# Prompt stick-breaking attention: operands and outputs turned in the unused columns of the diagonal steps' score slots

## The chip, the cores and the metric

One core of a Trainium2 chip runs the whole kernel. The metric is device time of one execution in microseconds. The engines are TensorE (PE in the profile, its weight loads PEld), VectorE (DVE), ScalarE (ACT), GpSimd (POOL) and SyncE (SP), which issues most transfers. Each works through its own instructions in order and waits for others by semaphores. TensorE writes its results to PSUM, a memory of 8 banks with 512 float32 columns each per partition. The granted clock (PEclk) is a share of TensorE's full speed: 1.0 is 2.4 GHz, 0.5 is 1.2 GHz.

## The reference

One step of a decoder layer, with a prompt of 2048 tokens and 8 samples of 4 new tokens. The input is projected to two groups of heads; the first attends by stick-breaking, the second in dilated windows; then come an output projection and a gated embedding. The part at hand is stick-breaking attention over the prompt, 8 heads of 64:

```python
def _stick_breaking(q, k, v, q_pos, k_pos, bias):
    z = jnp.einsum('bqhd,bkhd->bhqk', q, k).astype(jnp.float32) / math.sqrt(HEAD_DIM)
    z = z + bias.astype(jnp.float32)[None, :, None, None]
    mask = (k_pos[None, :] < q_pos[:, None])[None, None]
    log_1m = jnp.where(mask, jax.nn.log_sigmoid(-z), 0.0)
    rest = lax.cumsum(log_1m, axis=3, reverse=True) - log_1m
    a = jnp.where(mask, jnp.exp(jax.nn.log_sigmoid(z) + rest), 0.0)
    return jnp.einsum('bhqk,bkhd->bqhd', a.astype(v.dtype), v)
```

For each query the weight of a key is its sigmoid times the product of (1 - sigmoid) over all keys between it and the query, which is a sum of softplus values in the exponent.

## The kernel before

`build` runs seven stages one after the other on the core: projection of mixer A, projection of mixer B, prompt stick-breaking, dilated prompt, sampled stick-breaking, dilated sample, merge. Between stages all engines meet. The change is in the third (function `stick_breaking_prompt`), in the helper that loads its operands, and in the line of the second stage that calls that helper.

The stage handles its 8 heads in 4 pairs (`PAIRS`). For a pair, the queries and keys of all 2048 positions lie as rows in the buffer `held`. They are turned by TensorE (a product with the identity matrix into PSUM), then ScalarE copies the result as a rounded high part `T_hi` and VectorE subtracts it for a low part `T_lo`. This is a **fill**. There are 4 fills a pair, each of 8 tiles of 128 x 128, two for the queries and two for the keys.

The scores are made transposed: keys on partitions, queries on columns. The queries are taken in 4 **quarters** of 512 (Q = 0 to 3). A quarter Q passes over the key tiles from its last one, j = 4Q + 3, down to 0: 4, 8, 12 and 16 **steps**, 40 a pair and 160 in all, numbered g. The first four steps of each quarter are its **diagonal**: there key tile j meets only the queries behind it, so columns from `first_col(g)` = 384, 256, 128 and 0 are used and those left of it are not.

A step g does the following, for both heads of the pair at once:

- TensorE, `score(g)`: bias and three products of high and low parts into a **slot** of `Z` (two banks, one for each head); on a diagonal also a mask.
- ScalarE: `exp(g)` (the line called L812 below), then `ln(g)` (L817). VectorE: `softplus(g, h)` (L739). GpSimd: `high(g)`, the softplus rounded (L697). VectorE: `low(g, h)`, the rest (L745).
- TensorE, `sums(g)`: adds the softplus sums within the key tile into the same slot (L894, L898); `totals(g)`: the totals of the tile for the later steps (L909).
- ScalarE, `weights(g)`: exponential of the slot (L824), which frees it; `left(g)`: exponential of the totals (L832).
- TensorE, `weigh(g)`: weights times values into `L` (L922). VectorE, `scale(g)` and `add(g)`: adds it to the quarter's output in `acc`.

When a quarter is done its output is turned back by four transposes (an output **turn**, L864), which ScalarE copies to `o_out` (the put-out, L803).

`Z` has three slots (`ZS = 3`), six of the eight PSUM banks; `total` and `L` hold the other two. Before the change, a list `SLOTS` holds steps, fills and turns in one order, and the n-th entry takes slot n % 3. Every engine runs through this list in a loop over k: it starts entry k + 2 and finishes entry k. So scores run two entries ahead of sums, and a fill or turn is an entry like a step. A fill of the next pair stands before steps 8, 16, 24 and 32 of a pair (`FILL_AT`), the four of the first pair before step 0; a turn stands five steps behind the last step of its quarter (`TURN_AT`). A new entry waits until the slot's last user has been read (`wait_free`): for a step until its weights are out (`a_done`).

SP issues the loads. The rows of the next pair are loaded into `held` when all four fills of the pair are turned. The first pair's are loaded at the end of the projection stage, before the loads of its last item.

## Time and profile before

| | |
|---|---|
| timed runs | 3353.92, 3348.5, 3353.68 us; median 3353.68 us |
| profiled execution, span from first to last instruction | 3201.8 us |
| TensorE busy | 2899.0 us (91%) |
| VectorE busy | 1654.1 us (52%) |
| ScalarE busy | 1464.1 us (46%) |
| GpSimd busy | 632.9 us (20%) |
| mean granted clock of TensorE | 0.953 |
| prompt stick-breaking, first to last compute instruction | 801.6 to 1489.2 us |

The span holds only the time between the first and the last instruction; the timed runs are longer by what lies around it. For the profiled execution the page gives the span alone. The shares are means over seven stages with different limits, so only what is read inside the stage says something of this change. In a row of the timeline the first number is the start and the second the duration, both in microseconds, of the instructions named; x8 means eight of one kind in a row, and the brackets give the idle time of the engine before it and what ended it.

### The profile page before, as it was taken

The numbers are of one execution on the slowest core, as the hardware profiler recorded it, in microseconds if no ns is written. First come the engines' busy times: TensorE is split into PE (matmuls) and PEld (weight loads), VectorE is DVE, ScalarE is ACT, GpSimd is POOL, SyncE is SP. The second block draws the span as 40 slices with busy tenths as digits, with TensorE's granted clock in tenths as the row PEclk, the third lists the DMA queues.
The fourth block names the chain that finished last, engine by engine and source line by source line (L and its number), as shares of the span: only waits on it lengthen the run. The fifth ranks groups of instructions, "written<-read, shape, count | busy, mean of one in ns | idle before, by whom it ended". The sixth has DMA issues, their size and how long they took to land. (4 is left out here: it accounts for less than half of the span.)

```text
span 3201.8 us, 46967 instructions
## 1 busy us (share of the span) xinstructions
PE 2899.0 (91%) x17542; PEld 2086.6 (65%) x17542; DVE 1654.1 (52%) x2702; ACT 1464.1 (46%) x2550; POOL 632.9 (20%) x908
## 2 busy tenths in 40 slices
PE   7999989999899999998999958888888874799998
PEld 5888858887555555555888845555555441588887
DVE  2000032222687878887666636555555434666663
ACT  3222131111577777776556625555555423333332
POOL 0000001111222222221123343333333200000000
PEclk9999999999899999999999979999999886899999
DMA  6655765555201010103323339999999885333321
GB/s 203 210 206 210 242 207 184 183 209 184 82 1 40 1 40 1 44 8 93 80 55 81 90 117 421 420 420 420 420 420 420 334 343 212 130 105 104 105 85 41
DMA packets 209508, 574.12 MB, mean 179 GB/s; under 512 B 39840, under 2 KB 108928, under 8 KB 173472
## 3 DMA queue, kind: packets, MB, share of 16 engines
q0 software_dynamic: 45568, 348.22, 27.7%
q1 hardware_dynamic: 163744, 223.27, 21.3%
q8 instruction: 125, 2.05, 0.3%
q14 instruction: 71, 0.58, 0.1%
HBM read 494.67 MB, written 143.73 MB: 199 GB/s over the span
## 5 line engine op out<-in xcount | busy, mean ns | idle before, releaser
L1535 DVE COPY sbs_kT<-sbs_ps_T 128x512 f32<-128x512 f32 x256 | 270.6, 1092 | 270.2 <-PE sbs_ps_T L1697 269.9
L495 PE MATMUL proj_ps_G<-proj_w_hi,proj_xT_hi 128*128 128x512 f32 x1024 | 400.2, 391 | 1.6 <-DVE proj_xT_lo L352 1.6
L499 PE MATMUL proj_ps_G<-proj_w_hi,proj_xT_lo 128*128 128x512 f32 x1024 | 398.8, 389 | 0.0
L497 PE MATMUL proj_ps_G<-proj_w_lo,proj_xT_hi 128*128 128x512 f32 x1024 | 398.7, 389 | 0.0
L434 ACT ACTIVATE proj_out<-proj_ps_G,proj_stat 128x512 f32<-128x512 f32 (+1 forms) x136 | 93.4, 689 | 581.7 <-PE proj_ps_G L499 575.9
L1697 PE MATMUL sbs_ps_T<-held,sbs_k_ring 128*128 128x128 f32 x2048 | 279.6, 292 | 43.2 <-ACT sbs_kT L1618 39.7
L1697 PEld LDWEIGHTS sbs_ps_T<-held,sbs_k_ring 128*128 128x128 f32 x2048 | 247.5, 152 | 86.6 <-ACT sbs_kT L1618 42.1
L697 POOL CAST sbp_sp_hi<-sbp_sp 128x512 fp32r<-128x512 f32 (+3 forms) x320 | 172.3, 553 | 505.3 <-DVE sbp_sp L739 497.2
L1618 ACT ACTIVATE sbs_kT<-sbs_ps_T 128x512 f32<-128x512 f32 x256 | 260.0, 1115 | 5.7 <-PE sbs_ps_T L1697 5.1
L739 DVE SCALAR_TENSOR_TENSOR sbp_sp<-sbp_Z,sbp_el 128x512 f32<-128x512 f32 (+3 forms) x320 | 179.9, 603 | 121.6 <-ACT sbp_el L817 121.2
L495 PEld LDWEIGHTS proj_ps_G<-proj_w_hi,proj_xT_hi 128*128 128x128 f32 x1024 | 192.5, 188 | 41.6 <-DVE proj_xT_lo L352 1.8
L499 PEld LDWEIGHTS proj_ps_G<-proj_w_hi,proj_xT_lo 128*128 128x128 f32 x1024 | 192.3, 188 | 40.0
L497 PEld LDWEIGHTS proj_ps_G<-proj_w_lo,proj_xT_hi 128*128 128x128 f32 x1024 | 192.5, 188 | 39.4
L812 ACT ACTIVATE sbp_el<-sbp_Z 128x1024 f32<-128x1024 f32 (+3 forms) x160 | 143.5, 897 | 139.1 <-PE sbp_Z L885 138.3
L745 DVE TENSOR_TENSOR sbp_sp_lo<-sbp_sp,sbp_sp_hi 128x512 fp32r<-128x512 f32 (+3 forms) x320 | 198.6, 660 | 4.0 <-POOL sbp_sp_hi L697 1.4
L352 DVE TENSOR_TENSOR proj_xT_lo<-proj_ps_T,proj_xT_hi 128x512 fp32r<-128x512 f32 (+1 forms) x34 | 21.2, 662 | 320.1 <-ACT proj_xT_hi L421 320.0
L1465 POOL DMA_INDIRECT sbs_v_ring<-in_cache_v_sb,sbs_rows x128 | 120.3, 940 | 330.2 <-PE sbs_O L1730 300.4
L1230 ACT ACTIVATE dil_sc<-dil_Z,dil_keep 128x256 f32<-128x256 f32 (+1 forms) x384 | 162.8, 451 | 3.6 <-DVE dil_keep L1161 3.6
L922 PE MATMUL sbp_L<-sbp_a,sbp_v_all 128*64 128x512 f32 (+3 forms) x640 | 153.8, 558 | 5.2 <-DVE sbp_acc L755 3.3
L824 ACT ACTIVATE sbp_a<-sbp_Z 128x1024 f32<-128x1024 f32 (+3 forms) x160 | 143.4, 896 | 29.9 <-PE sbp_Z L898 25.8
L817 ACT ACTIVATE sbp_el<-sbp_el 128x1024 f32<-128x1024 f32 (+3 forms) x160 | 147.8, 924 | 0.9
L1161 DVE TENSOR_REDUCE dil_keep<-dil_Z 128x2 f32<-128x512 f32 (+1 forms) x160 | 103.0, 685 | 87.0 <-PE dil_Z L1292 87.0
(291 smaller groups left out, 5798.8 us busy)
## 6 DMA issues: line engine op xcount, KB each, us to landing
out_k_win_s<-in_cache_k_win POOLq DMA_DIRECT2D x16, 2044.0 KB
out_v_win_s<-in_cache_v_win POOLq DMA_DIRECT2D x16, 2044.0 KB
dls_k_in<-in_cache_k_win SPq DMA_DIRECT2D x16, 1024.0 KB, 10.4
dls_v_in<-in_cache_v_win SPq DMA_DIRECT2D x16, 1024.0 KB, 14.3
proj_out<-in_w_in SPq DMA_DIRECT2D x28, 512.0 KB, 4.9
merge_o<-scratch_o_dil SPq DMA_DIRECT2D x48, 256.0 KB, 4.6
proj_x_in<-in_x_prompt SPq DMA_DIRECT2D x16, 512.0 KB, 4.2
scratch_xT_hi<-proj_xT_hi SPq DMA_DIRECT2D x16, 512.0 KB, 4.7
```

Source lines behind the costliest of these rows:

```text
L495: nc.tensor.matmul(ps_G[0:n, g, :], xT_hi[:, slot, k, 0:n], w_hi[:, k, cols], start=(k == 0), stop=False)
L497: nc.tensor.matmul(ps_G[0:n, g, :], xT_hi[:, slot, k, 0:n], w_lo[:, k, cols], start=False, stop=False)
L499: mm = nc.tensor.matmul(ps_G[0:n, g, :], xT_lo[:, slot, k, 0:n], w_hi[:, k, cols], start=False, stop=(k == KC - 1))
L697: nc.gpsimd.tensor_copy(sp_hi[:, b, h, c:512], sp_[:, b, h, c:512]).then_inc(hi_done, 1)
L739: nc.vector.scalar_tensor_tensor(out=sp_[:, b, h, c:512], in0=Z[:, z(g), h, c:512], scalar=LINEAR, in1=el[:, b, h, c:512], op0=ALU.max, op ...
L745: nc.vector.tensor_tensor(sp_lo[:, b, h, c:512], sp_[:, b, h, c:512], sp_hi[:, b, h, c:512].bitcast(F32), ALU.subtract).then_inc(lo_done, 1)
L817: nc.scalar.activation(el[:, g % 2, :, c:512], el[:, g % 2, :, c:512], ACT.Ln, bias=1.0).then_inc(ln_done, 1)
L922: mm = nc.tensor.matmul(L[h * DH:(h + 1) * DH, c:512], v_all[:, j, p * P + h * DH:p * P + (h + 1) * DH], a[:, g % 2, h, c:512], start=True ...
L1230: e = nc.scalar.activation(sc[:, g % 2, h, cols], Z[:, 2 * (g % 2) + h, cols], ACT.Exp, bias=keep[:, b % 2, 0, x + n, h:h + 1], accum_out= ...
L1535: nc.vector.tensor_copy(by_lane(kT[:, j, :, :])[:, :, i, :], ps_T[:, x % TB, :].rearrange("p (a n) -> p a n", a=PAIRS)).then_inc(kT_odd, 1)
L1618: nc.scalar.activation(by_lane(kT[:, j, :, :])[:, :, i, :], ps_T[:, x % TB, :].rearrange("p (a n) -> p a n", a=PAIRS), ACT.Copy).then_inc( ...
L1697: tr = nc.tensor.transpose(ps_T[:, x % TB, pr * P:(pr + 1) * P], k_ring[:, q % RING, i, pr * P:(pr + 1) * P], ident[:, :])
```

## The change

- **Steps alone take slots.** Step g has slot g % 3, and the loop over k runs over steps only. `SLOTS`, `FILL_AT` and `TURN_AT` are gone.
- **Fills go by quarters of the sequence, in pieces.** A quarter (4 tiles of queries and 4 of keys) is turned during the diagonal two quarters earlier (`EARLY = 2`), also across pairs: 1 tile of each in the diagonal's first step, 2 in the second, 1 in the third, in the columns just left of `first_col(g)` of that step's own slot, before its scores are issued. ScalarE copies the piece after `exp(g)`, VectorE subtracts after `softplus(g, 1)`. `sums(g)` additionally waits for that subtraction. There are 14 such quarters. The first two quarters of the first pair are turned before step 0, in slots 1 and 2.
- **Turns** of quarter n stand in the first step of quarter n + 2, in columns 0 to 255 of both banks. The last two stand behind the last step.
- **Waits.** The first score of a quarter waits only for its own quarter's operands. TensorE starts the first fills when the identity matrix is loaded, on a semaphore of its own.
- **Loads.** A quarter of `held` is reloaded for the next pair once that quarter has been turned: two loads of 256 KB for each quarter in place of four of 512 KB for a pair. The first pair's are eight loads instead of four. The stores of the outputs stay as they were, on two semaphores.

```diff
@@ load_prompt_pair -> load_prompt_quarter
-    for n in range(2):
-        tiles = slice(n * TILES // 2, (n + 1) * TILES // 2)
-        for i in range(2):
-            sp.dma_start(qk_in[:, i, tiles, :], rows[i][:, tiles, p * P:(p + 1) * P]).then_inc(loaded[2 * i + n], 16)
+    tiles = slice(Q * TILES // 4, (Q + 1) * TILES // 4)
+    for i, src in enumerate((t["q_sb"], flat(t["k_sb_p"]))):
+        rows = src.rearrange("(n p) c -> p n c", p=P)
+        sp.dma_start(qk_in[:, i, tiles, :], rows[:, tiles, p * P:(p + 1) * P]).then_inc(loaded[Q], 16)
@@ stick_breaking_prompt, the order
-    FILL_AT = {}
-    for p in range(PAIRS):
-        for f in range(FILLS):
-            FILL_AT.setdefault(0 if p == 0 else NP * (p - 1) + 8 * (f + 1), []).append(("fill", p, f))
-    TURN_AT = {closing(p, Q) + 5: ("turn", p, Q) for p in range(PAIRS) for Q in range(NQ)}
...
     def z(g):
-        return SLOT["step", g, None]
+        return g % ZS
+
+    def fills_to(n):
+
+        return min(n, EARLY) if n <= EARLY else EARLY + PIECES * (n - EARLY)
+
+    def fill_at(g):
+
+        p, Q, j, s = step(g)
+        n = quarter(g) + EARLY
+        if s >= PIECES or n >= NALL:
+            return None
+        t0 = QT * (n % NQ)
+        a, b = ((0, 1), (1, 3), (3, 4))[s]
+        return fills_to(n) + s, n // NQ, t0 + a, t0 + b
+
+    def fill_cols(g):
+
+        c = first_col(g)
+        p, piece_p, a, b = fill_at(g)
+        return slice(c - (b - a) * P, c)
+
+    def turn_at(g):
+
+        n = quarter(g) - EARLY
+        return n if step(g)[3] == 0 and n >= 0 else None
@@ SP
+            for n in range(NALL):
+                if n + NQ < NALL:
+                    sp.wait_ge(turned, fills_to(n + 1))
+                    load_prompt_quarter(sp, t, held, (n + NQ) // NQ, n % NQ, pair_loaded)
+                if n + NQ == NALL:
+                    sp.wait_ge(turned, fills_to(NALL))
+                    load_dilated_qk(sp, t, held, 0, dil_qk_loaded)
+                done = n - 2 * EARLY
+                if done >= 0 and done % NQ == NQ - 1:
+                    p = done // NQ
+                    sp.wait_ge(o_copied, done + 1)
+                    sp.dma_start(o_rows[:, :, p * P:(p + 1) * P], o_out[:, p % 2, :, :]).then_inc(o_stored[p % 2], 16)
@@ VectorE, the loop
+            for n in range(EARLY):
+                first_fill(n)
+            for k in range(-2, G):
+                x = k + 2
+                if x < G:
                     softplus(x, 0)
                     softplus(x, 1)
-                if weighed is not None:
-                    scale(weighed)
+                    if fill_at(x) is not None:
+                        fill(x)
+                if k > 0:
+                    scale(k - 1)
...
@@ ScalarE, the loop
+                if x < G:
                     exp(x)
+                    if turn_at(x) is not None:
+                        put_out(turn_at(x), z(x))
+                    if fill_at(x) is not None:
+                        fill(x)
+                if k >= 0:
+                    weights(k)
+                if x < G:
                     ln(x)
...
@@ TensorE
             def score(g):
                 c, (p, Q, j, s) = first_col(g), step(g)
-                wait_free(pe, ("step", g, None))
-                if g % NP == 0:
-                    pe.wait_ge(turn_lo, FILLS * p + FILLS)
+                wait_free(pe, g)
+                if turn_at(g) is not None:
+                    turn_out(turn_at(g), z(g))
+                if fill_at(g) is not None:
+                    fill(g)
+                if s == 0:
+                    pe.wait_ge(turn_lo, fills_to(quarter(g) + 1))
...
             def sums(g):
                 c, b = first_col(g), g % 2
+                if fill_at(g) is not None:
+                    pe.wait_ge(turn_lo, fill_at(g)[0] + 1)
...
-            pe.wait_ge(consts, 48)
+            pe.wait_ge(ident_loaded, 16)
+            for n in range(EARLY):
+                first_fill(n)
+            pe.wait_ge(set_up, 14 + PAIRS)
```

How the instructions move: TensorE before, from a turn in pair 1's second quarter on (L864 is the turn, L894 to L909 sums and totals of the steps, L922 the values, L876 and L885 scores).

```order
L864 MATMUL sbp_Z<-sbp_ident,sbp_acc 128x128 x4
L894 MATMUL sbp_Z<-sbp_sp_hi,sbp_suf_r 128x512 x2
L898 MATMUL sbp_Z<-sbp_sp_lo,sbp_suf_r 128x512 x2
L909 MATMUL sbp_total<-sbp_sp_hi,sbp_all_r 128x512 x2
L909 MATMUL sbp_total<-sbp_sp_lo,sbp_all_r 128x512 x2
L922 MATMUL sbp_L<-sbp_a,sbp_v_all 64x384 x2
L876 MATMUL sbp_Z<-sbp_bias_row,sbp_lift_r 128x512 x2
L885 MATMUL sbp_Z<-sbp_T_hi 128x512 x2
L885 MATMUL sbp_Z<-sbp_T_hi,sbp_T_lo 128x512 x2
L885 MATMUL sbp_Z<-sbp_T_lo,sbp_T_hi 128x512 x2
L876 MATMUL sbp_Z<-sbp_bias_row,sbp_lift_r 128x512 x2
L885 MATMUL sbp_Z<-sbp_T_hi 128x512 x2
```

The turn stands alone between two steps' sums, with no scores beside it, and then follow scores of two steps (L876 to L885, and L876 again) with no sums between. TensorE after, the first step of a quarter's diagonal in pair 1 (L892 is the turn, L886 a piece of a fill, L908 to L917 the scores, L928 to L943 sums and totals, L956 the values):

```order
L892 MATMUL sbp_Z<-sbp_ident,sbp_acc 128x128 x4
L886 MATMUL sbp_Z<-sbp_ident,held 128x128 x2
L908 MATMUL sbp_Z<-sbp_bias_row,sbp_lift_r 128x128 x2
L912 MATMUL sbp_Z<-sbp_later_r,sbp_ident_r 128x128 x2
L917 MATMUL sbp_Z<-sbp_T_hi 128x128 x2
L917 MATMUL sbp_Z<-sbp_T_hi,sbp_T_lo 128x128 x2
L917 MATMUL sbp_Z<-sbp_T_lo,sbp_T_hi 128x128 x2
L928 MATMUL sbp_Z<-sbp_sp_hi,sbp_suf_r 128x384 x2
L932 MATMUL sbp_Z<-sbp_sp_lo,sbp_suf_r 128x384 x2
L943 MATMUL sbp_total<-sbp_sp_hi,sbp_all_r 128x384 x2
L943 MATMUL sbp_total<-sbp_sp_lo,sbp_all_r 128x384 x2
L956 MATMUL sbp_L<-sbp_a,sbp_v_all 64x256 x2
```

Turn and piece stand directly before the scores of a step, and each step's scores are followed by the sums of the one two steps back.

ScalarE before, in the same part of the first pair (L796 copies a fill, L803 puts a turn out, L812 and L817 are exponential and logarithm of the scores, L824 the weights, L832 the totals):

```order
L817 ACTIVATE sbp_el<-sbp_el 128x1024
L832 ACTIVATE sbp_E<-sbp_total 128x256
L796 ACTIVATE sbp_T_hi<-sbp_Z 128x1024
L824 ACTIVATE sbp_a<-sbp_Z 128x2x384
L832 ACTIVATE sbp_E<-sbp_total 128x384
L803 ACTIVATE sbp_o_out<-sbp_Z 128x512
L824 ACTIVATE sbp_a<-sbp_Z 128x1024
L832 ACTIVATE sbp_E<-sbp_total 128x512
L812 ACTIVATE sbp_el<-sbp_Z 128x1024
L817 ACTIVATE sbp_el<-sbp_el 128x1024
L812 ACTIVATE sbp_el<-sbp_Z 128x1024
L817 ACTIVATE sbp_el<-sbp_el 128x1024
```

Around the fill and the turn no scores come in (L812 is missing for two entries). ScalarE after, a diagonal's first three steps (L828, L833 exponential and logarithm, L820 the put-out, L813 pieces of a fill, L840 the weights, L848 the totals):

```order
L828 ACTIVATE sbp_el<-sbp_Z 128x2x128
L820 ACTIVATE sbp_o_out<-sbp_Z 128x512
L813 ACTIVATE sbp_T_hi<-sbp_Z 128x2x128
L840 ACTIVATE sbp_a<-sbp_Z 128x1024
L833 ACTIVATE sbp_el<-sbp_el 128x2x128
L848 ACTIVATE sbp_E<-sbp_total 128x512
L828 ACTIVATE sbp_el<-sbp_Z 128x2x256
L813 ACTIVATE sbp_T_hi<-sbp_Z 128x2x256
L840 ACTIVATE sbp_a<-sbp_Z 128x1024
L833 ACTIVATE sbp_el<-sbp_el 128x2x256
L828 ACTIVATE sbp_el<-sbp_Z 128x2x384
L813 ACTIVATE sbp_T_hi<-sbp_Z 128x2x128
```

Put-out and pieces stand between the exponential of a step's scores and the weights of the step two before it.

## Rows read from the trace of the kernel before

**Rows 1.** Windows of all engines, busy us (count), PEclk, DMA share, GB/s, stage's middle
```profile
1300.00:1400.00 100.00, 97.74 (x529) 56.90 (x529) 80.89 (x160) 73.73 (x102) 26.60 (x51) 1.00 0.14 38
```

**Rows 2.** Timeline of ScalarE (start, us): first exponential of each pair, then the last
```profile
815.03 0.38 ACT L812 ACTIVATE sbp_el<-sbp_Z 128x256 f32<-128x256 f32 x1 [2.65 <-PE sbp_Z L885]
...
981.63 0.38 ACT L812 ACTIVATE sbp_el<-sbp_Z 128x256 f32<-128x256 f32 x1 [0.61 <-PE sbp_Z L885]
...
1151.10 0.38 ACT L812 ACTIVATE sbp_el<-sbp_Z 128x256 f32<-128x256 f32 x1 [0.62 <-PE sbp_Z L885]
...
1319.53 0.38 ACT L812 ACTIVATE sbp_el<-sbp_Z 128x256 f32<-128x256 f32 x1 [0.61 <-PE sbp_Z L885]
...
1475.75 1.03 ACT L812 ACTIVATE sbp_el<-sbp_Z 128x1024 f32<-128x1024 f32 x1 [0.64 <-PE sbp_Z L885]
```

**Rows 3.** Timeline of TensorE, one undisturbed full step of the last pair
```profile
1470.29 0.50 PE L876 MATMUL sbp_Z<-sbp_bias_row,sbp_lift_r 64*128 64x512 f32 x2
...
1471.42 0.73 PE L894 MATMUL sbp_Z<-sbp_sp_hi,sbp_suf_r 128*128 128x512 f32 x2
...
1472.46 0.62 PE L909 MATMUL sbp_total<-sbp_sp_hi,sbp_all_r 128*128 128x512 f32 x2
...
1474.49 0.50 PE L876 MATMUL sbp_Z<-sbp_bias_row,sbp_lift_r 64*128 64x512 f32 x2
```

**Rows 4.** Timeline of TensorE, a fill and an output turn in pair 1
```profile
1009.52 1.09 PE L856 MATMUL sbp_Z<-sbp_ident,held 128*128 128x128 f32 x8
1010.37 0.59 PE L894 MATMUL sbp_Z<-sbp_sp_hi,sbp_suf_r 128*128 128x384 f32 x2
...
1012.66 0.66 PE L864 MATMUL sbp_Z<-sbp_ident,sbp_acc 128*128 128x128 f32 x4
...
1020.86 1.39 PE L894 MATMUL sbp_Z<-sbp_sp_hi,sbp_suf_r 128*128 128x512 f32 x2 [1.82 <-POOL sbp_sp_hi L697]
```

**Rows 5.** Windows after such a place, the granted clock eighth
```profile
1020.00:1030.00 10.00, 9.14 (x34) 4.77 (x34) 8.87 (x15) 7.63 (x9) 3.65 (x6) 0.83 0.01 2
```

**Rows 6.** Timeline of TensorE, an output turn alone in pair 3
```profile
1379.26 0.66 PE L864 MATMUL sbp_Z<-sbp_ident,sbp_acc 128*128 128x128 f32 x4
1379.67 0.59 PE L894 MATMUL sbp_Z<-sbp_sp_hi,sbp_suf_r 128*128 128x384 f32 x2
...
1381.83 0.65 PE L922 MATMUL sbp_L<-sbp_a,sbp_v_all 128*64 128x256 f32 x4 [0.37 <-DVE sbp_acc L755]
...
1388.42 0.86 PE L894 MATMUL sbp_Z<-sbp_sp_hi,sbp_suf_r 128*128 128x512 f32 x2
...
1390.26 0.63 PE L909 MATMUL sbp_total<-sbp_sp_hi,sbp_all_r 128*128 128x512 f32 x2
```

**Rows 7.** Groups by line in the stage: busy us, mean ns, idle before
```profile
L730 DVE TENSOR_TENSOR sbp_T_lo<-sbp_Z,sbp_T_hi 128x1024 fp32r<-128x1024 f32 x16 | 19.2, 1213 | 0.0
L796 ACT ACTIVATE sbp_T_hi<-sbp_Z 128x1024 fp32r<-128x1024 f32 x16 | 16.4, 1028 | 8.5 <-PE sbp_Z L856 8.4
L803 ACT ACTIVATE sbp_o_out<-sbp_Z 128x512 f32<-128x512 f32 x16 | 9.7, 606 | 8.0 <-PE sbp_Z L864 8.0
```

**Rows 8.** Timeline of VectorE, one read of 256 columns from PSUM
```profile
1016.34 0.41 DVE L758 TENSOR_TENSOR sbp_LE<-sbp_L,sbp_E 128x256 f32<-128x256 f32 x1
```

**Rows 9.** Timeline, a diagonal's second step in pair 3: three engines
```profile
1371.28 1.02 ACT L824 ACTIVATE sbp_a<-sbp_Z 128x1024 f32<-128x1024 f32 x1 [0.49 <-PE sbp_Z L898]
...
1372.36 0.19 PEld L876 LDWEIGHTS sbp_Z<-sbp_bias_row,sbp_lift_r 64*128 64x128 f32 x2 [0.98 <-ACT sbp_a L824]
...
1372.86 0.75 DVE L739 SCALAR_TENSOR_TENSOR sbp_sp<-sbp_Z,sbp_el 128x256 f32<-128x256 f32 x2 [2.23 <-ACT sbp_el L817]
```

**Rows 10.** Timeline of the stage's start
```profile
808.96 4.69 DVE L730 TENSOR_TENSOR sbp_T_lo<-sbp_Z,sbp_T_hi 128x1024 fp32r<-128x1024 f32 x4
...
813.79 0.33 PE L876 MATMUL sbp_Z<-sbp_bias_row,sbp_lift_r 64*128 64x128 f32 x2 [2.46 <-DVE sbp_T_lo L730]
```

**Rows 11.** Windows of the stage's start, the granted clock eighth
```profile
816.00:830.00 14.00, 14.00 (x60) 10.70 (x56) 8.05 (x17) 7.54 (x13) 3.47 (x8) 0.51 0.58 146
```

212 lines of the change are left out of this document (95 added, 117 removed).

## The prediction

> **What bounds the kernel now.** The change touches one of seven stages, the prompt stick-breaking (lines L661 to L943), so I read the timeline for its ends first, then the windows inside it, then single steps of each engine. The execution profiled spans 3201.8 us and the three timed runs have a median of 3353.68 us; the 151.9 us between lie outside the span and I take them unchanged, so each microsecond saved in the span is one off the median. In the middle of the stage TensorE is busy 97.7 of 100 us at full clock, VectorE 81, ScalarE 74, GpSimd 27, DMA at 0.14 [rows 1]. TensorE bounds it: a full undisturbed step takes 4.20 us, 1.13 for the scores, 1.04 for the sums, 2.03 for totals and values, with no gap between them [rows 3]. What can be won is therefore TensorE's own work and the places at which its row is broken.
>
> Those places show in the length of the four pairs of heads, which do the same 40 steps each. From the starts of the first exponentials [rows 2] pair 0 takes 981.63 - 815.03 = 166.6 us, pair 1 169.5, pair 2 168.4, and pair 3, to the last exponential plus one step of 4.2, 160.4. Pairs 1 and 2 hold four fills and four output turns, pair 3 four turns and no fill. So four fills cost (169.5 + 168.4)/2 - 160.4 = 8.5 us. Their transposes alone are 1010.37 - 1009.52 = 0.85 us each [rows 4], 3.4 a pair; the other 5.1 are disturbance. Its form is seen where a fill and a turn come close together: each takes one of three score slots and one turn of the loop, the scores that should run two steps ahead are caught up in one heap, and TensorE then stands 1.82 us before the sums of line L894, for GpSimd's rounded softplus [rows 4]. In the ten microseconds behind it the granted clock is 0.83 [rows 5], part of them at the lower level of 1.2 GHz.
>
> A turn alone costs 0.41 us of transposes (1379.26 to 1379.67), then 0.37 before the value products, and its sums take 1390.26 - 1388.42 = 1.84 us [rows 6] where an undisturbed step has 1472.46 - 1471.42 = 1.04 [rows 3]: 0.37 + 0.80 = 1.17 us of disturbance.
>
> **The change part by part.** Pieces of a fill now stand inside the scores of a diagonal's first three steps, and the turn inside the first. No entry takes a slot or a turn of the loop, so scores stay two steps ahead.
>
> Removed: 5.1 us a pair for the fills' disturbance in pairs 0 to 2 and 1.17 for each turn, 3 in pair 0 and 4 in the others.
>
> Kept: the transposes. 14 quarters of eight stand in the diagonals, four in each of pairs 0 to 2 and two in pair 3, which had none: 2 x 0.85 = 1.7 more there. Pair 0 has one turn fewer (0.41 less), since a turn comes two quarters after its own.
>
> Added: ScalarE copies three pieces (256, 512, 256 columns) in place of one of 1024 for a quarter. A read of 256 takes 0.38 [rows 2], one of 512 0.61 and one of 1024 1.03 [rows 7]: 1.37 for 1.03. VectorE subtracts in three too: 0.41 for 256 columns [rows 8], 1.21 for 1024 [rows 7], by a straight line 0.68 for 512, together 1.5 us. TensorE has no part in either, so the question is whether they delay something that it waits for. The worst step is a diagonal's second, where the 512 columns come. There ScalarE sits idle 0.49 us before the exponential of the weights, and TensorE's next score waits for exactly that exponential: its weight load stood 0.98 us for L824 [rows 9]. The copy of 0.61 goes into that idle 0.49 and pushes 0.12 through. Behind the waiting score on TensorE's queue stand the sums of the step before and the value products, so the delay is passed on whole. In the first step the exponential covers 256 columns only, so a put-out of 0.61 and a copy of 0.38 lie where a full step has 1.03 of exponential. VectorE has 2.23 us idle before its softplus of the second step [rows 9] and gets 0.68 + 0.41 = 1.1 us more by the end of the third; its softplus and low parts are late by what is left of ScalarE's delay plus this, and the sums that read them come two steps on. The trace of before has no copy inside a diagonal, so this cost has two ends: nothing, if every copy falls into such idle time, and 1.37 + 1.5 = 2.9 us a quarter, if each is on the way. I take 0.6, near the lower end, since both idle times measured are about as long as the work put into them. For 14 quarters that is 8.4 us.
>
> Pair by pair, with waits of 2.4 for four quarters: pair 0: 166.6 - 5.1 - 3.5 - 0.4 + 2.4 = 160.0, gain 6.6. Pairs 1 and 2: 160.4 + 3.4 - 4.7 + 2.4 = 161.5, gains 8.0 and 6.9. Pair 3: 160.4 - 4.7 + 1.7 + 1.2 = 158.6, gain 1.8. Sum 23.3.
>
> The start. Before, four subtractions of 1.17 us each (4.69 for four from 808.96) precede the first score, which waits for the last of them until 813.79 [rows 10]. Now the first score needs the first quarter's, after VectorE's same set-up: 3 x 1.17 = 3.5 us sooner. That TensorE waits for the identity matrix alone helps nothing, because VectorE's set-up ends the wait. The clock is open here. From 816 to 830 it was 0.51, the lower level [rows 11], after TensorE had stood 2.46 us [rows 10]. With the first work sooner and shorter, the low stretch may end early or last from the first score to 830. In low clock half the work is done: at 829.8 before had done 2.3 + 6.9 = 9.2 us of full-clock work since 813.8. Low until 814 from 810.3, the new kernel gets there at 821.3, gain 8.5; low until beyond 828, at 828.6, gain 1.2. I take 3.5 and keep both ends.
>
> The end. Two turns instead of one stand behind the last step; the first lies while ScalarE waits for sums, and costs its own 0.41.
>
> Transfers: the loads of the next pair come in quarters, each as soon as the same quarter of this pair has been turned; the first are used two quarters later, all others four, and the windows show the DMA at 0.14 [rows 1]. SP queues the store of a pair behind one of these loads; the next user of that output buffer comes two pairs later. Nothing is charged. At the end of the projection stage eight loads of half the size stand in place of four, ahead of the last item's own loads on SP's queue; the bytes are the same, and I take 0, with 2 us as the upper end.
>
> Sum: 23.3 + 3.5 - 0.4 = 26.4 us; 3353.7 - 26.4 = 3327.3 us.
>
> Where the Trainium skill speaks against this. The rows show a short stand of TensorE followed by a clock of 0.83 [rows 5]. The Trainium skill, TensorE: Matmul & The Clock Gate, section "A second HAM failure mode: psum-queue depth-cycling", says that short idles between groups of matmuls can make the clock swing between its levels even where no idle is long. In this trace the diagonals of pair 3 have such short stands and the clock stays at 1.00 beside them [rows 1], so it doesn't bind for them; if the copies lengthen them, it is the third rival below.
>
> **The rivals.** First, ScalarE's copies are all on the way, VectorE's not: 14 x 1.37 = 19.2 in place of 8.4, so 3338 us. For it: the score waits for L824 in the very step that gets the longest copy. Against it: the idle of 0.49.
>
> Second, slower. The loop turns on a chain: score, exponential, put-out, copy, weights, next score in that slot, and VectorE's subtraction stands before its scaling and low parts. If nothing of it is covered, each of 14 quarters pays 2.9 and 14 put-outs 0.61 each, 40.6 + 8.5 = 49.1 in place of 8.4: 3368 us. It decides from (26.4 + 8.4)/14 = 2.5 us a quarter. Against it: 0.49 and 2.23 us idle in front of just these instructions, and TensorE's 4.2 a step against VectorE's lower load in the diagonals.
>
> Third, the clock. If each of 16 diagonals now got a window of 0.83 as behind a fill and turn, 1.7 us each, 27 us go and the time is 3354: no change. For it only that the stands lie closer together.
>
> Fourth, a greater gain: no waits added and the low clock at the start ends early. 8.4 + 3 or so more, 3316 us.
>
> **How the numbers follow.** Forecast 0.70, with a range of its own of 3320 to 3336; ScalarE on the way 0.12; greater gain 0.09; no change by the clock 0.04; slower 0.05. A measurement of this kernel tells about 0.2% from no change, 6.7 us. The forecast, the first rival and the fourth lie on the faster side, together 0.91; I give 0.90 for faster, 0.05 for no change and 0.05 for slower. The predicted time is 3327; the range 3315 to 3341 takes in the cases but the last two.
>
> **What would show it.** Pair lengths between first exponentials near 160, 161.5, 161.5 and 159 us; no wait of TensorE of over 1 us for GpSimd in the stage after the start; full clock from the first diagonals on to the end of pair 3; first score at about 810.3. The forecast is wrong if the diagonals' steps grow by more than 0.6 us beyond their transposes, to be seen as TensorE waiting for the weights' exponential or VectorE's low part there, or if pairs 1 and 2 stay over 165 us.

## The result and the profile after

The changed kernel takes 3326.28 us (median of 4 runs, 3323.17 to 3332.23), the kernel before beside it on the same chip 3351.6 (4 runs, 3348.5 to 3353.92). The ratio is 0.9931 with a 95% interval of 0.9909 to 0.9952, so 16 to 31 us less. The forecast of 3327 us stands. Some of the terms behind it do not, and one sentence was plainly wrong. I begin with that one.

**The span before was not a usual one.** I put the 151.9 us between the span of 3201.8 us and the median outside the span. The changed kernel's profiled run has a span of 3330.1 us and a time of 3332.23: 2.1 us lie outside. A second profile of the unchanged kernel spans 3349.0. The difference is in a later stage, the sampled stick-breaking. Its key turns in the first profile of before, in the changed kernel and in the second profile of before (each row gives one group of instructions: shortest, median and longest duration in ns, start of the first and end of the last):

```profile
L1697 PE MATMUL sbs_ps_T<-held,sbs_k_ring x2048: 272/273/473, 1918.3 to 2539.9; 128*128 128x128 f32 x187
```
```profile
L1732 PE MATMUL sbs_ps_T<-held,sbs_k_ring x2048: 272/273/477, 1902.9 to 2669.6; 128*128 128x128 f32 x187
```
```profile
L1697 PE MATMUL sbs_ps_T<-held,sbs_k_ring x2048: 272/273/477, 1913.8 to 2686.3; 128*128 128x128 f32 x187
```

The same 2048 products took 622 us once and 767 and 772 us in the others. The windows of the same 550 us, of the first profile of before and of the changed kernel (columns as in [rows 1]), show the transfers beside them, 420 against 341 GB/s:

```profile
1950.00:2500.00 550.00, 475.61 (x3782) 299.21 (x3774) 307.89 (x391) 287.36 (x342) 220.58 (x224) 0.96 1.01 420
```
```profile
1950.00:2500.00 550.00, 416.10 (x3020) 272.77 (x3021) 256.07 (x314) 241.88 (x273) 164.83 (x176) 0.84 0.85 341
```

So one profiled execution can be 150 us off the timed ones in a stage that has nothing to do with the change. The terms of the prediction were read inside the changed stage, and that is why they survived.

**Pairs.** The first exponential of each pair and the last one (timeline of ScalarE), which answer to [rows 2]:

```profile
812.16 0.38 ACT L828 ACTIVATE sbp_el<-sbp_Z 128x256 f32<-128x256 f32 x1 [4.41 <-PE sbp_Z L917]
...
972.97 0.38 ACT L828 ACTIVATE sbp_el<-sbp_Z 128x256 f32<-128x256 f32 x1 [1.43 <-PE sbp_Z L917]
...
1135.54 0.38 ACT L828 ACTIVATE sbp_el<-sbp_Z 128x256 f32<-128x256 f32 x1 [1.43 <-PE sbp_Z L917]
...
1298.10 0.38 ACT L828 ACTIVATE sbp_el<-sbp_Z 128x256 f32<-128x256 f32 x1 [1.43 <-PE sbp_Z L917]
...
1453.29 1.03 ACT L828 ACTIVATE sbp_el<-sbp_Z 128x1024 f32<-128x1024 f32 x1 [0.65 <-PE sbp_Z L917]
```

The pairs take 160.8, 162.6, 162.6 and (to the last exponential plus 4.2) 159.4 us, where 160.0, 161.5, 161.5 and 158.6 were forecast. The middle of the stage, against [rows 1]; the second row is for the start, below:

```profile
1300.00:1400.00 100.00, 98.60 (x541) 57.76 (x540) 79.66 (x162) 73.60 (x107) 25.54 (x50) 1.00 0.14 38
...
812.00:825.00 13.00, 13.00 (x54) 9.29 (x52) 5.73 (x15) 6.57 (x14) 2.25 (x6) 0.50 0.74 227
```

TensorE bounds the stage still. Over the whole span the page has

```profile
PE 2939.2 (88%) x17542; PEld 2124.0 (64%) x17542; DVE 1658.2 (50%) x2730; ACT 1477.5 (44%) x2578; POOL 620.7 (19%) x908
```

where before TensorE was busy 2899.0 us. That is no added work of this size: the clock was lower in the later stage, 0.84 against 0.96 in the windows above, and the second profile of the unchanged kernel, with 0.83 there, has 2949.5 us. Now a diagonal's first two steps in the timeline of TensorE, with the fill pieces (L886), the turn (L892), the bias (L908), the mask (L912) and the first score product (L917):

```profile
1067.81 0.66 PE L892 MATMUL sbp_Z<-sbp_ident,sbp_acc 128*128 128x128 f32 x4
1068.30 0.38 PE L886 MATMUL sbp_Z<-sbp_ident,held 128*128 128x128 f32 x2
1068.61 0.33 PE L908 MATMUL sbp_Z<-sbp_bias_row,sbp_lift_r 64*128 64x128 f32 x2
1068.87 0.44 PE L912 MATMUL sbp_Z<-sbp_later_r,sbp_ident_r 128*128 128x128 f32 x2
1069.24 0.33 PE L917 MATMUL sbp_Z<-sbp_T_hi 64*128 64x128 f32 x2
1069.40 0.28 PE L917 MATMUL sbp_Z<-sbp_T_hi,sbp_T_lo 64*128 64x128 f32 x2
...
1072.79 0.66 PE L886 MATMUL sbp_Z<-sbp_ident,held 128*128 128x128 f32 x4
1073.38 0.39 PE L908 MATMUL sbp_Z<-sbp_bias_row,sbp_lift_r 64*128 64x256 f32 x2
...
1076.92 0.44 PE L886 MATMUL sbp_Z<-sbp_ident,held 128*128 128x128 f32 x2
1077.28 0.45 PE L908 MATMUL sbp_Z<-sbp_bias_row,sbp_lift_r 64*128 64x384 f32 x2
```

The three pieces take 0.31, 0.59 and 0.36 us from their start to that of the next product, 1.26 together; eight transposes in one block take 0.85 [rows 4]. Two transposes behind four others cost 0.31, while the eight in a block cost 0.11 each. I read the surplus as a price at each place where TensorE goes from a product on all 128 rows (written `128*128`) to one on 64 rows (`64*128`) or back; two runs below test it. It can be seen between products that wait for nothing: bias to mask 0.26, mask to score 0.37, and score to score, where nothing changes, 0.16. A wait for results in the same columns doesn't explain it: the bias products write none of the piece's columns and yet start 0.31 behind it.

And the copies? ScalarE in that second step, and TensorE's weight load behind it:

```profile
1075.24 0.59 ACT L813 ACTIVATE sbp_T_hi<-sbp_Z 128x512 fp32r<-128x512 f32 x1
1075.84 1.02 ACT L840 ACTIVATE sbp_a<-sbp_Z 128x1024 f32<-128x1024 f32 x1
...
1076.91 0.20 PEld L886 LDWEIGHTS sbp_Z<-sbp_ident,held 128*128 128x128 f32 x2 [0.98 <-ACT sbp_a L840]
```

The copy lies in the idle 0.49 of [rows 9], the exponential of the weights starts 0.01 us behind it, just as the sums end, and TensorE's stand is the same 0.98 as before. The copies are covered, and the wait that was feared did not come. Another one did, once in each of pairs 1 to 3: the turn in the first step of the second quarter stands 0.56 us for VectorE's last addition, since the first quarter between has only four steps.

```profile
987.76 0.63 PE L892 MATMUL sbp_Z<-sbp_ident,sbp_acc 128*128 128x128 f32 x4 [0.56 <-DVE sbp_acc L780]
```

### The profile page after: what moved, and what is told of

Same layout as the page of the kernel before. It is cut to its first block and busy times, and to the rows that moved or that the text cites. A ratio compares the mean times of both kernels' runs of the same rounds, so it can differ in the third digit from the quotient of the medians.

```text
span 3330.1 us, 47096 instructions
## 1 busy us (share of the span) xinstructions
PE 2939.2 (88%) x17542; PEld 2124.0 (64%) x17542; DVE 1658.2 (50%) x2730; ACT 1477.5 (44%) x2578; POOL 620.7 (19%) x908
## 5 line engine op out<-in xcount | busy, mean ns | idle before, releaser
L1732 PE MATMUL sbs_ps_T<-held,sbs_k_ring 128*128 128x128 f32 x2048 | 319.2, 315 | 62.2 <-ACT sbs_kT L1653 30.1
L1732 PEld LDWEIGHTS sbs_ps_T<-held,sbs_k_ring 128*128 128x128 f32 x2048 | 281.3, 167 | 109.5 <-issue 53.7
L1653 ACT ACTIVATE sbs_kT<-sbs_ps_T 128x512 f32<-128x512 f32 x256 | 271.0, 1102 | 102.3 <-PE sbs_ps_T L1732 84.6
L828 ACT ACTIVATE sbp_el<-sbp_Z 128x1024 f32<-128x1024 f32 (+3 forms) x160 | 143.9, 899 | 150.2 <-PE sbp_Z L917 149.0
L956 PE MATMUL sbp_L<-sbp_a,sbp_v_all 128*64 128x512 f32 (+3 forms) x640 | 152.3, 554 | 0.9 <-DVE sbp_LE L770 0.9
L840 ACT ACTIVATE sbp_a<-sbp_Z 128x1024 f32<-128x1024 f32 (+3 forms) x160 | 143.5, 897 | 9.8 <-PE sbp_Z L932 3.7
L833 ACT ACTIVATE sbp_el<-sbp_el 128x1024 f32<-128x1024 f32 (+3 forms) x160 | 147.7, 923 | 0.0
```

Of the source, the lines that this page charges most:

```text
L833: nc.scalar.activation(el[:, g % 2, :, c:512], el[:, g % 2, :, c:512], ACT.Ln, bias=1.0).then_inc(ln_done, 1)
L956: mm = nc.tensor.matmul(L[h * DH:(h + 1) * DH, c:512], v_all[:, j, p * P + h * DH:p * P + (h + 1) * DH], a[:, g % 2, h, c:512], start=True ...
L1653: nc.scalar.activation(by_lane(kT[:, j, :, :])[:, :, i, :], ps_T[:, x % TB, :].rearrange("p (a n) -> p a n", a=PAIRS), ACT.Copy).then_inc( ...
L1732: tr = nc.tensor.transpose(ps_T[:, x % TB, pr * P:(pr + 1) * P], k_ring[:, q % RING, i, pr * P:(pr + 1) * P], ident[:, :])
```

## The experiments

The steps' intervals below are differences between starts of the steps' exponentials (L828 in the changed kernel, L812 before) in the timeline of ScalarE; pair 3 is counted to the last one plus 4.2. The times of different runs are compared by their ratios to the kernel before, timed beside each.

**The kernel before, once more.**

> The kernel before, unchanged, run and profiled again. Theory A (the profiled execution of before was not typical: a stage outside the change, the sampled stick-breaking, ran in 643 us there and in 796 us in the trace of after): the span is now within 5 us of the timed 3351 us, that stage takes about 796 us, and the prompt stick-breaking stage has the same length as in the first trace, 665 us from the first exponential to the last plus one step. Theory B (as the prediction had it: 152 us lie outside the span): span about 3202 us again with a time of about 3351 us.

Ratio 0.9997 (0.9988 to 1.0007). The span is 3349.0 us for a run of 3350.8, as theory A has it; the stage, meant to take the same 665 us, took 660.9. Its pairs are 166.3, 167.1, 167.1 and 160.4 us. So the four fills of a pair cost 6.7 us in pairs 1 and 2 and not the 8.5 read from [rows 2]. TensorE and the window around the place of [rows 4, 5]:

```profile
1007.25 1.09 PE L856 MATMUL sbp_Z<-sbp_ident,held 128*128 128x128 f32 x8
...
1010.39 0.66 PE L864 MATMUL sbp_Z<-sbp_ident,sbp_acc 128*128 128x128 f32 x4
...
1018.62 1.10 PE L894 MATMUL sbp_Z<-sbp_sp_hi,sbp_suf_r 128*128 128x512 f32 x2 [1.81 <-POOL sbp_sp_hi L697]
```
```profile
1016.00:1026.00 10.00, 7.96 (x38) 4.17 (x36) 8.58 (x14) 8.41 (x10) 3.65 (x6) 1.00 0.01 2
```

The stand of 1.81 us (idle time of TensorE) is there again, the low clock is not. It is not absent from this execution, though. In pair 0 the clock falls behind both such stands, the first of them here:

```profile
851.00:863.00 12.00, 12.00 (x51) 6.14 (x50) 10.06 (x19) 8.09 (x11) 3.65 (x6) 0.86 0.00 0
```

Each execution has six such stands, two in each of pairs 0 to 2. The clock fell behind four of them in the first profile and behind two in the second. In the changed kernel, and in each of the next three runs, no window of 10 us between 836 and 1446 shows less than 1.00.

**The turns alone in the diagonals**, fills in slots of their own:

```diff
-    TURN_AT = {closing(p, Q) + 5: ("turn", p, Q) for p in range(PAIRS) for Q in range(NQ)}
+    def turn_at(g):
+        n = NQ * step(g)[0] + step(g)[1] - 2
+        return n if step(g)[3] == 0 and n >= 0 else None
...
+                if turn_at(g) is not None:
+                    turn_out(turn_at(g), z(g))
```

> The kernel before with only the output turns moved into the first step of a quarter's diagonal, two quarters later, as in the change; the fills keep slots of their own before steps 8, 16, 24 and 32. Theory A (a fill costs 2.1 us on the mean mainly because turns in slots of their own stand near it: 3.7 and 2.4 us where a turn follows, 1.2 and 0.7 where none does): pairs 1 and 2 fall from 169.5 and 168.4 to about 161.3 us, pair 3 to about 157; 3326 us, as good as the whole change. Theory B (each entry in a slot of its own has its own price, whatever stands beside it): turns give 0.9 each, pairs 1 and 2 take about 165.4 us, pair 3 about 157; 3338 us.

3335.8 us, ratio 0.9941 (0.9925 to 0.9958). Pairs 159.6, 162.3, 162.2, 156.8. Pairs 1 and 2 are nearer to theory A (161.3) than to B (165.4); the ratio lies between the two forecasts, whose times were reckoned from the longer pairs of the first profile. In pairs 1 and 2 this move alone reaches the changed kernel (162.6).

**The fills alone in the diagonals**, turns in slots of their own five steps behind their quarter:

```diff
+    TURN_AT = {closing(n) + 5: ("turn", n) for n in range(NALL)}
+    for g in range(G):
+        if g in TURN_AT:
+            SLOTS.append(TURN_AT[g])
+        SLOTS.append(("step", g))
...
```

> The changed kernel with the output turns back in slots of their own, five steps behind their quarter; fills in the diagonals, start and loads as changed. Theory A and B agree here on the fills, which cost 1.27 us a quarter in the diagonals as in the trace of after, with no turn beside them; turns cost again 0.9 more each: pairs 1 and 2 about 165.5 us, pair 3 about 163; 3340 us. If fills inside the diagonals disturb a turn that follows as a fill in a slot does, pairs 1 and 2 stay near 168.

3353.08 us, ratio 0.9992 (0.9981 to 1.0004): no change. Pairs 164.4, 165.9, 165.9, 162.9. The pairs came as expected (165.5 and 163), the time of 3340 us did not: it too was reckoned from the first profile, while against the second the four pairs are only 1.7 us shorter.

**Fills away from turns**, both in slots of their own:

```diff
-            FILL_AT.setdefault(0 if p == 0 else NP * (p - 1) + 8 * (f + 1), []).append(("fill", p, f))
+            FILL_AT.setdefault(0 if p == 0 else NP * (p - 1) + (12, 20, 24, 32)[f], []).append(("fill", p, f))
```

> The kernel before with two of a pair's four fills put elsewhere: before steps 12 and 20 in place of 8 and 16, so that no fill has an output turn one or two entries behind it. All entries keep slots of their own, nothing else changes. Theory A (closeness of fill and turn makes most of the loss): 4.2 us less in each of pairs 0 to 2, pairs 1 and 2 near 164.8 us, no window with a granted clock under 1.0 after the start, 3339 us. Theory B (a slot's own price): pairs stay at 168 to 169.5, 3351 us.

3344.55 us, ratio 0.9963 (0.9949 to 0.9977). Pairs 161.3, 164.1, 164.1, 160.4. Theory A meant 164.8 and 3339 us, which is a ratio of 0.996; B's 168 to 169.5 is out.

The four give a price list, with the second profile for the kernel before. Each row is a stretch of four steps of pair 1, in us (sums are of the unrounded intervals):

| stretch | kernel | intervals | sum | above plain |
|---|---|---|---|---|
| behind the diagonal, plain | changed | 2.8 3.3 4.0 4.2 | 14.3 | |
| with a turn in its own slot | fills apart | 6.0 4.0 2.0 3.9 | 15.9 | 1.6 |
| with fill and turn, two slots | before | 9.4 2.0 2.0 4.9 | 18.3 | 4.0 |
| diagonal, plain | before | 4.2 4.3 3.8 3.8 | 16.0 | |
| with a turn in the slot's columns | turns alone | 4.8 4.3 3.8 3.7 | 16.6 | 0.6 |
| with turn and fill in pieces | changed | 5.0 4.9 4.1 3.8 | 17.8 | 1.8 |

A turn in a slot of its own costs 1.6, in the diagonal 0.6: 1.0 less, four times a pair; pair 3, which has no fill, shows 160.4 - 156.8 = 3.6. A fill close to a turn costs 4.0 - 1.6 = 2.4; alone, in a slot of its own, it costs 0.6 to 0.7 where the diagonal begins and 1.1 to 1.2 in full steps; in pieces behind a turn 1.2, and 1.4 in the run with the fills alone ((165.9 - 160.4)/4). That is why moving the fills alone gains next to nothing: 14 quarters at 1.4 are 19 us, 2.5 of them in pair 3, which had none (162.9 - 160.4), in place of the 20 (3 x 6.7) that the fills cost before. Setting fills and turns apart takes 3.0 us off a pair (167.1 to 164.1), as the list says: one fill of 2.4 becomes one of 0.6 at step 12 (8.1 3.5 1.3 3.8 is 16.6), the other one of 1.2 at step 20. Theory A, that the closeness costs, holds.

**Every copy of ScalarE twice**, the first into a spare buffer that nobody reads:

```diff
+                if e > EARLY:
+                    act.wait_ge(spared, e - EARLY)
+                nc.scalar.activation(spare[:, :, 0:(b - a) * P], Z[:, z(g), :, fill_cols(g)], ACT.Copy).then_inc(spared, 1)
```

> The changed kernel, in which ScalarE copies each piece of T_hi a second time, into a spare buffer that nobody reads, behind the first copy (42 copies more: 14 quarters by 0.38 + 0.59 + 0.38 us). It asks whether the copies stand on the way in the diagonal steps. Theory A (what the profile of the changed kernel shows: the copy at 1075.24 is over when the sums that the weights' exponential waits for are done, and the 0.4 to 0.6 us that a quarter with pieces costs is TensorE's own): there is about 0 us of cover left in the second step, where the copy ends within 0.1 us of the sums, and 0.4 us and more in the first and third, so the second copies cost the 0.59 us of the second step and nothing else: 14 x 0.59 = 8 us over the changed kernel, about 3334, pairs 0 to 2 longer by 2.4 us each. Rival B (each ScalarE copy is on the way, as the prediction's term for waits would have it with its upper end): 14 x 1.36 = 19 us, about 3345, pairs longer by 5.4. Rival C (ScalarE has slack everywhere in the diagonals): within 2 us of the changed kernel.

3335.9 us, ratio 0.996 (0.9945 to 0.9975), 9.7 us above the changed kernel's ratio; pairs 161.8, 164.5, 164.5, 160.6, so 1.9 for a full pair. The weight load behind the second step now stands

```profile
1079.32 0.20 PEld L891 LDWEIGHTS sbp_Z<-sbp_ident,held 128*128 128x128 f32 x2 [1.36 <-ACT sbp_a L845]
```

1.36 in place of 0.98: the first copy starts at 1077.27 and the next instruction 0.48 later, and 0.38 of that come through, once a quarter. The other two copies of the quarter cost nothing (intervals 5.0 4.9 4.5 3.8 for 5.0 4.9 4.1 3.8). Quarter 1, whose diagonal comes behind the short quarter 0, pays 0.3 more at its first step. The place is theory A's, the price smaller than its 0.59. The four pairs together are 5.9 us longer; the intervals of the two ratios leave room for that beside the 9.7. B's 19 us, or 5.4 a pair, is out.

**Every subtraction of VectorE twice**, likewise:

```diff
+                if e > EARLY:
+                    dve.wait_ge(spared, e - EARLY)
+                nc.vector.tensor_tensor(spare[:, :, 0:(b - a) * P], Z[:, z(g), :, fill_cols(g)],
+                                        T_hi[:, p % 2, :, cols].bitcast(F32), ALU.subtract).then_inc(spared, 1)
```

> The changed kernel, in which VectorE subtracts each piece a second time, into a spare buffer that nobody reads (42 subtractions more, 0.38 to 0.60 us each, about 1.4 us a quarter). Theory A (TensorE sets the pace of the diagonal steps): 0 to 0.3 us a quarter, so at most 4 us over the changed kernel. Rival B (VectorE's queue, which is the fullest after TensorE's, is the one that the pieces load): 14 x 1.4 = 20 us over it, about 3346, with TensorE's waits for sbp_T_lo or sbp_sp_lo longer by as much.

3335.42 us, ratio 0.9957 (0.9942 to 0.9971), 8.7 above the changed kernel's. Pairs 1 and 2 are 163.9, 1.3 longer, and pair 3 0.7. Pair 0 is 3.2 longer, most of it in steps 3 and 4, where the clock was still 0.50 from 824 to 829.9 in this execution. So the time is above theory A's 4 us and far below B's 20. A wait that the changed kernel doesn't have at this place stands in front of the third step's value products, for the scaled output that VectorE reads out of the same bank:

```profile
1083.28 1.08 PE L962 MATMUL sbp_L<-sbp_a,sbp_v_all 128*64 128x512 f32 x4 [0.24 <-DVE sbp_LE L776]
```

So VectorE's slack in the diagonals is used up with one more set of subtractions. The pairs make up 6.6 of the 8.7 us, and some 2 of these are the clock's.

**Mask before bias, bias cut in two.** Here the bias and mask of the diagonal's own 128 columns do not enter the result in three of four diagonal steps, so this run serves only to time the order.

```diff
-                for h in range(2):
-                    r = slice(h * DH, (h + 1) * DH)
-                    nc.tensor.matmul(Z[:, z(g), h, c:512], lift_r[r, :], bias_row[r, p, c:512], start=True, stop=False,
-                                     skip_group_check=True)
                 if diagonal(g):
                     for h in range(2):
-                        nc.tensor.matmul(Z[:, z(g), h, c:c + P], ident_r[:, :], later_r[:, :], start=False, stop=False,
+                        nc.tensor.matmul(Z[:, z(g), h, c:c + P], ident_r[:, :], later_r[:, :], start=True, stop=False,
                                          skip_group_check=True)
+                for h in range(2):
+                    r = slice(h * DH, (h + 1) * DH)
+                    for a, b in ((c, c + P), (c + P, 512)) if diagonal(g) else ((c, 512),):
+                        if a < b:
+                            nc.tensor.matmul(Z[:, z(g), h, a:b], lift_r[r, :], bias_row[r, p, a:b],
+                                             start=a > c or not diagonal(g), stop=False, skip_group_check=True)
```

> The changed kernel with another order of the products that begin a diagonal step: the two mask products (128 rows by 128 columns, like the transposes ahead of them) first, then the bias products (64 rows), so that TensorE changes between whole and half arrays once instead of three times; the bias product of the second to fourth diagonal step is cut in two for it (two more products of 64 rows each). Theory A (the changeover costs: 0.17 us with nothing to wait for stands ahead of the first bias product behind a transposition, and the same between bias and mask and between mask and score): 0.2 to 0.3 us a diagonal step less what the cut adds (about 0.1), so 64 steps x 0.1 to 0.2 = 6 to 13 us less than the changed kernel, 3313 to 3320. Rival B (the 0.17 us are the latency of the last transposition, which is paid in any order; the cut then costs its own): 0 to 5 us more than the changed kernel.

Ratio 0.9897 (0.9881 to 0.9913), 11 us under the changed kernel's. Pairs 153.8, 158.4, 158.4, 156.3.

**Mask before bias, whole**, with everything in the result (the diff is against the run before):

```diff
-                    for a, b in ((c, c + P), (c + P, 512)) if diagonal(g) else ((c, 512),):
...
+                    nc.tensor.matmul(Z[:, z(g), h, c:512], lift_r[r, :], bias_row[r, p, c:512], start=not diagonal(g), stop=False,
+                                     skip_group_check=True)
```

> The changed kernel with the two mask products first and the bias products behind them as one piece over all columns (the run with the bias product cut in two measured pairs of 158.3 us where the changed kernel has 162.5, and the steps between the diagonals alike). Its trace has the four cut bias products in 0.28 us before the first score product, against 0.16 to 0.22 for two uncut ones. Theory A (each change between products of 64 rows and of 128 rows costs about 0.15 us, whatever the order of the data): uncut, three diagonal steps of a quarter save 0.06 to 0.12 us more, so pairs of 157 to 157.6, 150 us/1000 of a per cent apart from that run by 3 to 5 us: a median about 14 us under the changed kernel's ratio, 0.988 to 0.989 of the kernel before. Rival B (the gain of the cut run comes from the cut, or from what it leaves out): pairs of 161 and more, ratio 0.992 or more.

(A pair 0.8 to 1.4 us shorter than in the cut run was meant, 3 to 5 us in all.) Ratio 0.9886 (0.9872 to 0.99), 3311.47 us. Pairs 152.2, 157.7, 157.7, 155.4: 0.7 under the cut run in pairs 1 and 2, and 4.9 under the changed kernel. In pair 0 it is 8.6, because the clock was back at 1.00 by 813 in this execution; 4 to 5 us a pair is the order's own. The same first step as above in its timeline of TensorE:

```profile
1052.64 0.66 PE L892 MATMUL sbp_Z<-sbp_ident,sbp_acc 128*128 128x128 f32 x4
1053.13 0.38 PE L886 MATMUL sbp_Z<-sbp_ident,held 128*128 128x128 f32 x2
1053.27 0.42 PE L908 MATMUL sbp_Z<-sbp_later_r,sbp_ident_r 128*128 128x128 f32 x2
1053.62 0.33 PE L912 MATMUL sbp_Z<-sbp_bias_row,sbp_lift_r 64*128 64x128 f32 x2
1053.78 0.28 PE L917 MATMUL sbp_Z<-sbp_T_hi 64*128 64x128 f32 x2
...
1057.28 0.66 PE L886 MATMUL sbp_Z<-sbp_ident,held 128*128 128x128 f32 x4
1057.69 0.42 PE L908 MATMUL sbp_Z<-sbp_later_r,sbp_ident_r 128*128 128x128 f32 x2
```

From the first piece to the first score product it is 1053.78 - 1053.13 = 0.65 us, before 1069.24 - 1068.30 = 0.94. The same products in an order with one change instead of three save 0.29. The pieces cost 0.14 and 0.41 now, in place of 0.31 and 0.59: with a product of the same height behind them it is 0.07 to 0.10 a transpose, no more than the 0.11 in the block of eight. Theory A holds, also in the size of the whole (0.988 to 0.989 was meant), and B is out.

**Fills before steps 12, 20, 24 and 32, turns in the diagonals.** The edit is that of the run with the turns alone and that of the fills away from turns, together.

> The kernel before, with only the outputs turned in the diagonal steps (as in the run that had this part alone, 3336), and the four operand fills of a pair, which keep slots of their own, ahead of steps 12, 20, 24 and 32 instead of 8, 16, 24 and 32. In that run's trace a fill cost 1.6 us ahead of step 8, 1.6 ahead of 16, 0.7 ahead of 24 (the first diagonal step of quarter 3) and 1.1 ahead of 32. Theory A (a fill costs least where the diagonal steps, which are shorter, come right behind it, and less late in the quarter than early): steps 12 and 20 cost 0.7 and 1.1, so 1.4 us a pair less, three pairs 4 us: about 3331.5, pairs 0 to 2 at 158.2, 160.9 and 160.9. Rival B (the differences between the four places are not the place's): the same 3335.8 within 2 us, the costs at 12 and 20 stay at 1.6.

3324.79 us, ratio 0.9921 (0.9909 to 0.9932). Pairs 161.9, 161.0, 161.0, 156.8: 1.3 under the run with turns alone in pairs 1 and 2, as theory A has it (160.9); pair 0 (158.2 expected) did not follow, since the clock was 0.50 from 814 to 834 in this execution. The fill before step 12 costs 0.7 (8.7 3.5 1.3 3.8), the one before 20 costs 1.2 (8.1 4.2 2.0 3.7 against four times 4.2). The intervals of the two ratios overlap, so in the time the gain isn't settled.

**Mask ahead as well**, that is, the kernel of the last run with the edit of the whole mask ahead:

> A version that takes from each run what gained: the kernel before, with the outputs turned in the diagonal steps, the operand fills in slots of their own ahead of steps 12, 20, 24 and 32, and the mask products ahead of the bias products. Its predecessor without the last part has pairs of 161.0 and a ratio of 0.9921. In the run with the mask first, the diagonal steps of pair 3, which hold no fills, took 4.4, 4.2, 3.6, 3.7 us where the changed kernel has 4.8, 4.3, 3.8, 3.7: 0.7 us a quarter, with the bias product cut in two. Theory A (the changeovers add up, and fills in a slot of their own have no part in them): 161.0 - 4 x 0.9 = 157.4, four pairs 14 us: ratio 0.988, the same within 2 us as the changed kernel with the mask first. Rival B (with slots of their own for the fills, TensorE has less to save in the diagonals, since it waits there for VectorE): less than 1 us a pair, ratio 0.991 or more.

Ratio 0.9891 (0.9877 to 0.9904), 3313.59 us. Pairs 157.1, 157.6, 157.7, 153.4. With the mask ahead, pieces and slots of their own for the fills come out alike in pairs 1 and 2; pair 3 is 2.0 us shorter without pieces (153.4 against 155.4). Theory A again.

**TensorE kept busy at the start**:

```diff
+            for x in range(14):
+                nc.tensor.transpose(L[:, x % 4 * P:(x % 4 + 1) * P], ident[:, :], ident[:, :])
             pe.wait_ge(set_up, 14 + PAIRS)
```

> The changed kernel, in which TensorE turns the identity 14 times into L's bank (which nobody reads then) between the first two fills and its wait for the constants, so that it is not idle from 806.7 to 809.0. It asks what the low clock of the first steps costs (granted clock 0.66 from 816 to 830, and 30.9 us from the end of the projections to the first exponential of quarter 1, as long as in the kernel before). Theory A (the idle stretch is what lowers the clock): quarter 0's intervals fall from 3.1, 3.1, 4.8 us to about 2.6, 2.6, 3.4, so the stage is 2 to 3 us shorter, ratio 0.9923 against the changed kernel's 0.9931, just at the edge of what can be told. Rival B (the clock falls whatever TensorE does there, as it fell in the kernel before too): pairs and start alike, ratio 0.993; the 14 transpositions lie in the wait.

Ratio 0.9918 (0.9904 to 0.9932), 3324.07 us. This execution comes to its stage later, so the window that answers to 812 to 825 of the changed kernel above, 13 us from the first exponential on, is

```profile
815.60:828.60 13.00, 12.45 (x90) 8.77 (x88) 9.17 (x23) 9.72 (x20) 3.47 (x8) 1.00 0.84 267
```

The granted clock is 1.00 (2.4 GHz) in place of 0.50 (1.2 GHz), with TensorE idle for 0.43 and 0.69 us ahead of its first pieces and scores instead of 2.34 and 0.44. The exponential of step 4 comes 24.7 us behind ScalarE's copy of the last projection product instead of 30.9. Other traces bear it out. The same 13 us show 0.50 in the changed kernel, in both runs with doubled copies and in the one with the fills alone, which start in the same way, and 1.00 in the run with both edits below. So theory A's mechanism is seen in two traces against four, and B's, that the clock falls whatever TensorE does, is out for them. The worth is not settled: the ratio is lower by some 4 us than the changed kernel's, but the two intervals overlap. And the idle stretch is not the whole story, since the run with the whole mask ahead also got to step 4 in 24.7 us without these transposes. Its clock fell to 0.50 too, but was back at 1.00 from 813.

**Mask ahead and kept busy**, both edits on the changed kernel:

> The changed kernel with both additions: the mask products ahead of the bias products, and the 14 transpositions that keep TensorE busy before the first scores. Alone they measured 0.9886 and 0.9918 of the kernel before, where the changed kernel measured 0.9931. Theory A (the two are independent): pairs of 157.7 us, 24 to 25 us from the end of the projections to the first exponential of quarter 1, ratio 0.9886 - 0.0013 = 0.987, some 3307 us. Rival B (the diagonal steps of quarter 0 are so much shorter with the mask first that the low clock ends early in any case, as in that run's trace, which also took 24.7 us there): no further gain, 0.9886.

Ratio 0.9859 (0.9842 to 0.9875), 3309.74 us against 3359.59 for the kernel before in that session. Pairs 150.9, 157.7, 157.7, 155.4, step 4 at 23.3 us. It is the lowest ratio measured, 0.7 points under the changed kernel. Theory A's 0.987 lies inside the interval, B's 0.9886 outside. But against the run with the mask ahead alone the two traces differ by only 1.4 us at the start and not in pairs 1 to 3, where the ratios differ by 9 us; their intervals overlap a little, so the second edit's worth beside the first stays open.

## Why the prediction was right, and where it was not

**The sum.** Forecast 26.4 us, measured 25.3 between the medians, 16 to 31 by the interval. Against the second profile of before the changed kernel's pairs together are 15.6 us shorter (660.9 to 645.3) and its first exponential 2.3 us earlier, counted from the end of the projections; against the first profile the pairs are 19.6 shorter. The forecast for the pairs was 23.3.

**Turns.** I took 1.17 us of disturbance off each. The list has 1.6 - 0.6 = 1.0, and pair 3 shows 3.6/4 = 0.9. Right, a little large.

**Fills.** This step was mis-sized and laid at the wrong door. I took 5.1 us a pair as the fills' own disturbance, removed by pieces. The number held 1.8 us of low clock behind such places in pairs 1 and 2 (8.5 against 6.7), which came in one execution and not in the other, and most of the other 3.3 belongs to two fills standing close to turns: moving these two away from the turns took 3.0 of it. The sentence that fills and turns close together make the heap was right, but I priced the two apart, and there the whole is not the sum of its parts. Fills alone measured 0.9992, turns alone 0.9941, together 0.9931. With the turns moved, the fills in pieces gain nothing more in pairs 1 and 2 (162.3 to 162.6).

**Waits.** I charged 0.6 us a quarter for ScalarE's and VectorE's copies. A quarter with a turn and pieces costs 1.8 above plain: 0.6 of the turn, 0.85 of the block of eight, and 0.35 to 0.4 more. So the size is near, the cause is not. It is TensorE, which pays at each change between full and half height; ScalarE's copies lie in idle time, as the same 0.98 shows. My reading of [rows 9], that they fill the idle 0.49 nearly exactly, was right: a doubled copy is at once on the way. The other part, that 0.12 us of the single one would be, was not. The 0.56 us of the turn that waits for VectorE was in no term.

**Pair 3.** Forecast 158.6, found 159.4; pieces cost it 2.6 (159.4 - 156.8), against 2.9 charged for transposes and waits. The rest is turns.

**The start.** The first score was forecast at 810.3 and came at 810.16:

```profile
810.16 0.47 PE L908 MATMUL sbp_Z<-sbp_bias_row,sbp_lift_r 64*128 64x128 f32 x2 [0.44 <-DVE sbp_T_lo L735]
```

The gain at the first score did not last: step 4's exponential comes 30.9 us behind ScalarE's copy of the last projection product, before 30.7 and 30.3. At 812 to 825 the clock is 0.50 while TensorE is busy throughout, and three steps of quarter 0 now hold pieces that are paid at that level. My lower end of 1.2 did not reckon with them; the term was near 0 in these traces.

**The end.** I charged 0.4 us for the second turn. From the last exponential to the last turn it is 12.2 us in all three traces, so it cost nothing, and TensorE's first product of the next stage comes 1.3 us sooner than in the second profile of before.

**Clock.** No window behind a diagonal shows less than 1.00 once the low clock of the start has ended at about 825 (not from the first diagonals on, as the prediction had it), so the third rival, and what the Trainium skill's page TensorE: Matmul & The Clock Gate has in "A second HAM failure mode: psum-queue depth-cycling", did not come to pass in the changed kernel: stands of 0.98 us at each diagonal leave the clock at 1.00 from 1300 to 1400 here. In the kernel before, a fall did follow six of the twelve stands of 1.8 us in two executions, and the change took those stands away. TensorE waits for GpSimd nowhere for more than 0.4 us in the stage, as forecast.

In all, pairs, start and end give 19 us against the second profile of before and 23 against the first, where 26.4 were forecast and the medians differ by 25. The interval of the ratio holds all of these. So the agreement to 1 us is partly luck. What was right is the mechanism, the two heaps of fill and turn and the steps that stay two ahead; the term for the fills was too large (by its own terms 8.5 - 3.4 - 2.4 = 2.7 us a pair, where the fills moved alone gained 167.1 - 165.9 = 1.2), that for the turns alone too (4.7 against 3.6; in pairs with fills close by, the move gained 4.8), and that for the start was not there.
